# Two expert loops instead of one, extra weight slots at experts 17 to 19, GpSimd's table loads one expert ahead, and row spreads inside the third gather group

## What is computed

```python
def hier_moe(h, w_rg, b_rg, w_re, b_re, w_eg, w_eu, w_ed):
    p_grp = softmax(hf @ w_rg + b_rg)                 # 4 groups
    g_star = argmax(p_grp)
    e_logits = (hf @ w_re + b_re)                     # 4 x 8 experts
    top_l, top_i = lax.top_k(in_grp, 2)               # 2 of the group's 8
    combine = p_g * softmax(top_l)
    expert_ids = g_star * 8 + top_i
...
    def expert_block(args):                           # 32 experts, 1024 -> 256 -> 1024
        hdn = silu(xb @ w_eg[e]) * (xb @ w_eu[e])
        return hdn @ w_ed[e]
```

## Time and profile before

| | us |
|---|---|
| median of 3 runs | 1126.09 |
| the three runs | 1126.09, 1118.88, 1126.10 |
| the profiled execution | 1120.13 |
| its span, first to last instruction | 1118.3 |
| PE, PEld busy | 986.2, 623.1 |
| DVE, ACT, POOL busy | 385.6, 290.9, 71.1 |

### The profile page before, as it was taken

The page is one execution under the profiler, slowest core; times in us unless marked ns, Lnnn a source line. Parts: engine busy times, 40 slices in busy tenths (PEclk is TensorE's granted clock), DMA queues, the critical chain, the costliest instruction groups (busy, mean ns, idle before and its releaser), DMA issues.

```text
span 1118.3 us, 21941 instructions
## 1 busy us (share of the span) xinstructions
PE 986.2 (88%) x7694; PEld 623.1 (56%) x7695; DVE 385.6 (34%) x1083; ACT 290.9 (26%) x673; POOL 71.1 (6%) x145
## 2 busy tenths in 40 slices
PE   4799999999988898799789999999998898778885
PEld 2567677477854444344356767746786444334343
DVE  2127632213262232223242682231336133222224
ACT  2325554410131111111043456441013111011012
POOL 1112000000100000000001200000010000000000
PEclk9889998989999999999999999998999899999988
DMA  8993232997385999999994332299831499999951
GB/s 360 314 421 134 111 114 81 377 420 313 114 338 188 421 422 422 421 420 419 419 335 150 147 113 76 88 352 420 337 145 39 175 419 422 422 422 420 420 235 44
DMA packets 65429, 318.97 MB, mean 285 GB/s; under 512 B 6050, under 2 KB 27874, under 8 KB 28226
## 3 DMA queue, kind: packets, MB, share of 16 engines
q1 hardware_dynamic: 63408, 314.86, 70.3%
q10 hardware_dynamic: 1810, 2.51, 0.6%
q0 software_dynamic: 128, 0.40, 0.1%
HBM read 315.24 MB, written 2.51 MB: 284 GB/s over the span
## 4 chain that ended last, share of the span: by engine, by line
PE 67%; DMA 13%; DVE 8%; ACT 5%; issue 4%; SPq 1%; POOLq 1%; POOL 0%; ACTq 0%; DVEq 0%; PEldq 0%
PE ps L576 20%; DMA ring<-wstream 13%; PE ps L1058 9%; PE ps L658 7%; PE ps L1035 5%; PE ps L1048 4%; PE ps L1067 4%; PE ps L967 3%; PE ps L614 3%; PE ps L1038 2%; PE ps L832 2%; PE ps L724 1%; DVE work L1420 1%; ACT work L1242 1%; DVE top L1419 1%
## 5 line engine op out<-in xcount | busy, mean ns | idle before, releaser
L1058 PE MATMUL ps<-ring,h 128*32 128x512 f32 x896 | 117.2, 628 | 36.3 <-DMA ring<-wstream 28.5
L576 PE MATMUL ps<-h,ring 128*128 128x288 f32 x512 | 134.4, 417 | 0.7 <-ACT work L1172 0.7
L576 PE MATMUL ps<-work,ring 128*128 128x288 f32 x512 | 132.6, 418 | 2.5 <-DVE work L1510 2.5
L576 PEld LDWEIGHTS ps<-work,ring 128*128 128x128 f32 x512 | 98.5, 195 | 30.0 <-issue 3.4
L576 PEld LDWEIGHTS ps<-h,ring 128*128 128x128 f32 x512 | 97.2, 195 | 29.6 <-issue 4.1
L658 PE MATMUL ps<-h,ring 128*128 128x288 f32 x416 | 104.9, 413 | 4.3 <-ACT h L1182 2.4
L1306 ACT ACTIVATE mraw<-ps 128x512 f32<-128x512 f32 x64 | 38.2, 597 | 259.5 <-PE ps L1058 259.0
L658 PEld LDWEIGHTS ps<-h,ring 128*128 128x128 f32 x416 | 79.6, 193 | 28.7 <-issue 7.2
L1663 DVE COPY yb<-ps 128x256 f32<-128x256 f32 x64 | 27.2, 425 | 186.0 <-PE ps L1048 186.0
L1067 PEld LDWEIGHTS ps<-fold,mraw 128*128 128x128 f32 x512 | 62.0, 191 | 51.0 <-ACT mraw L1306 42.8
L1655 DVE SCALAR_TENSOR_TENSOR h<-h,rms 128x288 f32<-128x288 f32 x128 | 60.6, 515 | 75.1 <-issue 75.1
(11 more groups left out here) (248 smaller groups left out, 1025.0 us busy)
## 6 DMA issues: line engine op xcount, KB each, us to landing
ring<-wstream SPq DMA_DIRECT2D x272, 1024.0 KB, 16.2
work<-wstream SPq DMA_DIRECT2D x16, 1024.0 KB, 17.9
work<-pages SPq DMA_DIRECT2D x32, 192.0 KB, 3.4
work<-pages SPq DMA_DIRECT2D x32, 128.0 KB, 2.2
x<-x_in SPq DMA_DIRECT2D x1, 1152.0 KB, 5.2
out_y<-h ACTq DMA_DIRECT2D x2, 576.0 KB, 2.8
cs<-consts SPq DMA_DIRECT2D x1, 1026.0 KB, 9.7
out_vp<-work ACTq DMA_DIRECT2D x2, 256.0 KB, 3.2
```

The source lines that it names most:

```text
L576: last = mm(out, w[:, (k0 + k) * stride:(k0 + k) * stride + 128], rhs(k), start=(k == 0), stop=(k == n - 1))
L1058: last = mm(pgu[32 * c:32 * c + 32, :], xs[:, k, :], ws[k // 4][:, c * 512:(c + 1) * 512], start=(k < 4), stop=(k >= 4), skip_group_check= ...
```

## The change

`LATE` becomes 17 and a new `TAIL` 20. The extra pairs are now 51 to 58: all of experts 17 and 18, gate and up of 19. TensorE runs expert 0, then 1 to 16 in four passes of the first loop, 17 to 19 written out, and 20 to 31 in three passes of a second loop with the same four bodies. GpSimd reads an expert's two numbers into registers at the end of the previous expert, and those of expert 0 ahead of its waits for the gather; VectorE therefore fills the table's last column in both rows. The four spreads move from behind the third gather group into it, one behind every second of its first eight products.

```diff
-LATE = 1 + 5 * ROUND
+LATE = 1 + 4 * ROUND
+TAIL = LATE + 3
...
+            first_slot = g.alloc_register("pool_first_slot")
+            n_blocks = g.alloc_register("pool_expert_blocks")
...
                 route.wait(g, l)
+                def look_ahead(e):
+
+                    g.reg_mov(first_slot, g.value_load(table[0:1, 0, e], min_val=0, max_val=SLOTS))
+                    g.reg_mov(n_blocks, g.value_load(table[0:1, 1, e], min_val=1, max_val=MAXBLK))
+
+                look_ahead(slice(0, 1))
                 far_kept.wait(g, l)
...
                 with g.Fori(0, N_EXP) as e:
-                    first = g.value_load(table[0:1, 0, bass.ds(e, 1)], min_val=0, max_val=SLOTS)
-                    nblk = g.value_load(table[0:1, 1, bass.ds(e, 1)], min_val=1, max_val=MAXBLK)
-                    with g.Fori(0, nblk) as b:
+                    with g.Fori(0, g.snap(n_blocks, min_val=1, max_val=MAXBLK)) as b:
                         n = g.snap(seen, min_val=0, max_val=200)
-                        at = within(first + b * BLK)
+                        at = within(g.snap(first_slot, min_val=0, max_val=SLOTS) + b * BLK)
...
                         g.reg_add(seen, seen, 1)
+                    look_ahead(bass.ds(e + 1, 1))
...
+                def spread_row(i):
+
+                    ps = job(f"bc{i}")
+                    if i == 0:
+                        banks.wait_drained(pe, l, "rows")
+                    filled(mm(ps[:, 0:T], bc(ident[0:4, i:i + 1], [4, 128]), rows4, start=True, stop=True), f"bc{i}")
+
...
                             mm(outs[c][:, 0:T], hrow[:, tb, (k0 + c) * 128:(k0 + c + 1) * 128], sel[:, tb, part],
                                start=(tb == 0), stop=False, skip_group_check=True)
+                            if hf and k0 == 0 and c % 2:
+                                spread_row(2 * tb + c // 2)
...
                 gather(1, 0)
-                for i in range(4):
-                    ps = job(f"bc{i}")
-                    if i == 0:
-                        banks.wait_drained(pe, l, "rows")
-                    filled(mm(ps[:, 0:T], bc(ident[0:4, i:i + 1], [4, 128]), rows4, start=True, stop=True), f"bc{i}")
                 gather(1, FAR)
...
-                for e in range(LATE, N_EXP):
+                for e in range(LATE, TAIL):
                     expert(e, table[0:1, 1, e + 1:e + 2])
+                with pe.Fori(0, (N_EXP - TAIL) // ROUND) as er:
+                    for j in range(ROUND):
+                        expert(TAIL + j, table[0:1, 1, bass.ds(er * ROUND + TAIL + j + 1, 1)], er)
...
-                r(V.tensor_copy(table[:, 1, N_EXP:N_EXP + 1], cs[0:1, C_ONE:C_ONE + 1]))
+                r(V.tensor_copy(table[:, :, N_EXP:N_EXP + 1], cs[0:1, C_ONE:C_ONE + 2].unsqueeze(2)))
```

## The result

The changed kernel takes 1096.01 us (median of 4 runs, 1094.51 to 1098.80) against 1125.65 of the kernel before beside it (1118.88 to 1126.10): a ratio of 0.9753, 95% interval 0.971 to 0.980. The profiled execution took 1098.80 us (span 1097.0), the slowest of the four, and 21.3 us shorter than the profiled one of before.

What follows compares the result with a forecast made beforehand. Stream and TensorE take turns setting the pace, with code waits in late written-out experts. 6.8 + 3.85 + 13.9 - 1.0 + 1.3 + 1.2 = 26.0 us off 1120.13 gives 1094.1, plus 2: 1096 us, range 1087 to 1107.

Steps and rivals of the forecast that it cites:

- Code waits as the cause: In the late written-out experts, TensorE's "issue" idle is waiting for code; 6.6 us lost in layer 0, 13.7 in layer 1.
- The late experts: Up to expert 31, the stream sets the end again: gains 6.8 us in layer 0, 13.9 in layer 1, less 1.0.
- Behind expert 31 of layer 0: From expert 31 to the sums, the code wait and half clock after it go: 3.85 us gained.
- No loss in the new loop's first pass: Experts 17 to 23 fetch seven bodies without loss above the stream's 6.6 us cover; bounds 0 and 7.1 us.
- rival (a): The new loop's first pass stalls in full, layer 1's expert 31 7.1 us above the stream: 1103 us; chance 0.14.
- rival (d): Four bodies exceed TensorE's code memory, so each jump back of the new loop fetches anew: +32, 1152 us; chance 0.03.
- Spreads: Inside the third gather group they cost the same 2.1 us; the fourth group's 0.64 us wait goes, 1.3 us in all.
- GpSimd: At expert 1, copies start 1.6 to 1.7 us earlier, its wait falls to 0.6; counted 0.6 us per layer, 1.2 in all.
- Before expert 16: Up to expert 16 nothing changes: it starts at 452.80 us in layer 0 and 985.19 in layer 1.
- The sum: All gains together, 26.0 us off the profiled 1120.13 us: 1094.1 us.
- The two microseconds added for the median: The profiled run lay 6 us under the median, perhaps through code waits; 2 of the 6 were added, giving 1096 us.

Runs made afterwards that it cites:

- experiment 3: Changed kernel, extra slots back at 21 to 23: 1096.12 us; never-executed branch and inner loop left out of the kernel before: 1096.49 us, of the changed kernel: 1095.39 us.
- experiment 4: Kernel before with 133 more TensorE instructions, always jumped over, in layer 0 ahead of its first loop: 1113.88 us, ratio 0.9923.
- experiment 6: Changed kernel with each body's never-entered inner loop written twice: 1240.82 us, ratio 1.106; written four times: 1468.09 us, ratio 1.308.
- experiment 2: Kernel before with the extra slots at 17 to 19, experts 17 to 31 written out, no second loop: 1112.60 us, ratio 0.9923.
- experiment 1: Kernel before with one part of the change each: loops and slots' place 1099.05 us, GpSimd's loads 1121.24 us, spreads 1119.63 us.
- the short kernels: Bodies without the never-executed branch and inner loop: kernel before so shortened 1096.49 us, ratio 0.9768; changed kernel so shortened 1095.39 us, ratio 0.9750.

## Why the prediction was right

*Code waits as the cause.* Right, and shown: experiment 3 removes them by removing code that isn't executed, experiment 4 moves them by counted instructions, experiment 6 adds to them by adding such code.

*The late experts.* Forecast 6.8 + 13.9 - 1.0 = 19.7 us; the stretches from expert 16 to 31 gained 5.7 + 13.3 = 19.0. Of the form, too: pace 5.75 from 20 on, the stream again at the end (from 27 and not 28; from expert 16 to 31 the stream took 93.2 and 92.7 us where 37 x 2.49 is 92.1), 1.6 us of weight wait each.

*Behind expert 31 of layer 0.* Forecast 3.85, measured 3.86.

*No loss in the new loop's first pass.* Right in the outcome (no "issue" idle there in either layer), but the reason was too short. I argued that seven bodies had run clean in layer 0 before. The number of bodies isn't what counts; the place of the packets' borders is. In layer 0 the code of the seven bodies lies where that of 21 to 27 lay, to within three instructions, so the analogy held; in layer 1 the borders, by the count, happen to fall well, the last of the seven just in the executed part. Had they fallen as in experiment 2, I think that rival (a) would have been nearer; no run shows it. By the rule of the Trainium skill (Runtime: NRT & Kernel Launch, section Instruction fetch mechanics) that made rival (d), the loop should have fetched at every jump back; the trace has no packet from 500 to 557, so the measurement decides against it for a loop of four times 279 instructions. In experiment 6 the time goes as rival (d) has it: with four times 687 instructions packets come in every pass.

*Spreads, +1.3 us forecast.* Not shown in the time, and the reason was wrong. The step that failed was "they cost the same 2.1 us of TensorE"; changing between the two shapes costs 1.2 us a layer, more than the 0.5 us of wait that it saves. Layer 0 lost 0.7 us by it. In layer 1 expert 0 did come 1.0 us earlier, but through the clock of the fourth group, of which the forecast knew nothing (experiment 1 has both).

*GpSimd, +1.2 us forecast.* 1.0 and 0.4 us won at expert 1, and nothing at the end. The two copies came 1.4 and 1.2 us earlier behind ScalarE's last, not 1.6 to 1.7, and expert 1 still waits 1.19 us (0.6 forecast).

*Before expert 16.* The forecast had nothing changing there, but the profiled execution lost 3.7 us in layer 0, where the first pass of the first loop had starts 7.4, 8.6, 8.8 and 10.2 us apart from expert 1 on (7.4, 5.8, 9.0, 6.8 before). Its code is the same and lies at the same place in the program, and the starts differ from kernel to kernel with it (7.3, 8.4, 8.8, 7.1 with the slots at 21; 7.3, 8.7, 8.3, 7.6 with the spreads alone), so I can't put this down to the change; the cause is open. Layer 1's first pass is within the change's reach: its code lies 1111 instructions earlier, as layer 0 has four bodies fewer, and the starts went from 8.3, 5.8, 5.8 and 5.8 us to 7.2, 6.8, 7.0 and 9.0. That cost nothing, for the stream sets expert 16 there (105.69 us from expert 0 before, 105.75 now).

*The sum.* It said 26.0 us. The profiled executions differ by 21.3, of which 18.0 lie where the change could act: 22.8 won on the late experts (23.6 forecast, with the 3.85) and 4.8 lost elsewhere (2.5 won by the forecast).

*The two microseconds added for the median.* Beside the experiments the kernel before ran between 1115.0 and 1128.2 us in 51 executions, with medians from 1120.9 to 1123.4, so its profiled 1120.13 was in the middle, and the median of three, 1126.09, high. The medians in the section on the result differ by 29.6 us, with the kernel before high; loops and slots alone took 22.0 off the median beside them. The reason I gave for the 6 us, that they might lie in the code waits, has nothing for it. The sum alone gave 1094.1 us, 0.4 below the fastest of the four runs; that 1096 came out so closely is luck.

## What to carry to other kernels

Code that is jumped over is fetched all the same, and beside weights at full rate a packet of 256 instructions came every 6.3 to 7.7 us once TensorE waited for it, longer than the 5.75 us of a body; look at the instruction queue's packets by stretch when idle time stands under "issue" in groups that wait for nothing. A loop whose body stays in the engine's memory, or a body half as long, removes it equally. Before an expected gain is summed up, find which resource would set the end next: here the stream, 6.6 us behind what TensorE could do, so that neither an earlier start of expert 1 nor a cleaner first pass (the short kernels) showed in the time.

## What was not expected

- The loss per written-out expert isn't even but comes in stretches of about six bodies, set by 279 against 256 instructions; 133 instructions that are never executed moved them and changed the time by 0.8% (0.9923, interval 0.989 to 0.996).
- Products of 4 rows among products of 128 rows: 7.98 us for what took 7.31 when the four stood together. And yet layer 1's next group ran at full clock with them (4.12 us) and never without (5.5 to 5.8).
- Four bodies of 415 instructions (6.5 packets) ran without new packets in some passes and not in others of the same kernel: 1240.82 us against 1096.01.
- A first pass without waits (starts 5.75 us apart, in the short kernels) took nothing off the time that could be told from noise.
